# Four engines round the first weight unit, the mixing norm in two token parts, and token rows that start at 32 bytes

## The reference

```python
def rms_norm(x, g):
    xf = x.astype(jnp.float32)
    y = xf * lax.rsqrt(jnp.mean(xf * xf, axis=-1, keepdims=True) + EPS)
    return (y * g.astype(jnp.float32)).astype(x.dtype)

h = jnp.concatenate([meta, x], axis=1)
xn = rms_norm(h, norm_gains[layer, 0])
proj = xn @ w_in[layer]
...
mixed = (jax.nn.sigmoid(g_a) * y_a + jax.nn.sigmoid(g_b) * y_b) @ w_out[layer]
h = h + rms_norm(mixed, norm_gains[layer, 1])
xn = rms_norm(h, norm_gains[layer, 2])
u = causal_depthwise_conv(xn @ w_up[layer], conv_w[layer], conv_b[layer])
u_gate, u_val = jnp.split(u, 2, axis=-1)
ffn = (jax.nn.gelu(u_gate, approximate=True) * u_val) @ w_down[layer]
```

## Time and profile before

| | us |
|---|---|
| three runs, median (lowest to highest) | 2176.37 (2175.43 to 2178.03) |
| the profiled execution | 2177.4 |
| its span, first to last instruction | 2175.6 |
| TensorE busy in it | 2143.6 |
| VectorE / ScalarE / GpSimd busy | 994.2 / 756.6 / 1010.3 |
| TensorE's share of the chain that ended last | 82% |

### The profile page before, as it was taken

The page is one execution under the profiler, slowest core; times in us unless marked ns, Lnnn a source line. Parts: engine busy times, 40 slices in busy tenths (PEclk is TensorE's granted clock), DMA queues, the critical chain, the costliest instruction groups (busy, mean ns, idle before and its releaser), DMA issues.

```text
span 2175.6 us, 31348 instructions
## 1 busy us (share of the span) xinstructions
PE 2143.6 (99%) x12490; PEld 1848.4 (85%) x12490; DVE 994.2 (46%) x1459; ACT 756.6 (35%) x1018; POOL 1010.3 (46%) x825
## 2 busy tenths in 40 slices
PE   8999999999999999999999999999999999999998
PEld 7897999999999887888888788878788888888886
DVE  5144454379888207322200829671876442222027
ACT  4133455243222216322212415551336332222134
POOL 4322223455555547555544545254331555555444
PEclk9999999999999999999999999999999999999999
DMA  4321111212222223322222221114220222222222
GB/s 165 103 69 69 59 44 74 97 59 97 96 92 83 108 95 111 120 96 96 97 97 96 102 101 44 57 60 153 78 78 21 97 97 97 96 96 97 96 101 93
DMA packets 31950, 195.17 MB, mean 90 GB/s; under 512 B 3968, under 2 KB 4480, under 8 KB 10096
## 3 DMA queue, kind: packets, MB, share of 16 engines
q1 hardware_dynamic: 26352, 182.66, 23.4%
q10 hardware_dynamic: 5504, 11.18, 1.6%
HBM read 189.47 MB, written 4.23 MB: 89 GB/s over the span
## 4 chain that ended last, share of the span: by engine, by line
PE 82%; issue 7%; DVE 5%; POOL 4%; ACT 1%; DMA 0%; SPq 0%; DVEq 0%; POOLq 0%; ACTq 0%
PE ps L2377 72%; POOL wlo L709 4%; PE ps L2972 2%; DVE sqa L1527 1%; PE ps L3187 1%; PE ps L3171 1%; PE ps L3054 1%; DVE x2lo L1515 1%; PE ps L3107 1%; PE ps L2656 1%; PE ps L2679 0%; PE ps L3152 0%; PE ps L2715 0%; PE ps L3197 0%; DMA h<-h 0%
## 5 line engine op out<-in xcount | busy, mean ns | idle before, releaser
L709 POOL TENSOR_TENSOR wlo<-raw,whi 128x512 fp32r<-128x512 f32 (+2 forms) x820 | 1009.0, 1263 | 1139.4 <-ACT whi L775 1035.4
L775 ACT CAST whi<-raw 128x2048 fp32r<-128x2048 f32 x162 | 309.6, 1911 | 810.7 <-PE ps L2377 753.3
L2377 PE MATMUL ps<-x2hi,whi 128*128 128x512 f32 x1136 | 448.9, 395 | 1.2 <-DVE x2lo L1515 1.1
L2377 PE MATMUL ps<-x2hi,wlo 128*128 128x512 f32 x1136 | 442.6, 390 | 0.0
L2377 PE MATMUL ps<-x2lo,whi 128*128 128x512 f32 x1136 | 442.4, 389 | 0.0
L2377 PE MATMUL ps<-xhi,whi 128*128 128x256 f32 (+2 forms) x1336 | 271.5, 285 | 12.2 <-DVE xlo L1581 9.3
L2377 PE MATMUL ps<-xlo,whi 128*128 128x256 f32 (+2 forms) x1336 | 270.0, 284 | 0.0
L2377 PE MATMUL ps<-xhi,wlo 128*128 128x256 f32 (+2 forms) x1336 | 269.9, 283 | 0.0
L2377 PEld LDWEIGHTS ps<-x2hi,whi 128*128 128x128 f32 x1136 | 213.4, 188 | 49.6 <-issue 4.8
L2377 PEld LDWEIGHTS ps<-x2lo,whi 128*128 128x128 f32 x1136 | 213.5, 188 | 44.6 <-issue 1.7
L2377 PEld LDWEIGHTS ps<-x2hi,wlo 128*128 128x128 f32 x1136 | 213.3, 188 | 44.3
(11 more groups left out here) (472 smaller groups left out, 2759.9 us busy)
## 6 DMA issues: line engine op xcount, KB each, us to landing
raw<-wstream SPq DMA_DIRECT2D x170, 1024.0 KB, 4.8
h<-h SPq DMA_DIRECT2D x4, 528.0 KB, 8.7
ncb<-c_rows ACTq DMA_DIRECT2D x8, 256.0 KB, 3.5
ple_rows<-ple_out ACTq DMA_DIRECT2D x4, 512.0 KB, 4.0
bias<-bias_rows ACTq DMA_DIRECT2D x8, 256.0 KB, 4.6
ple<-ple_rows ACTq DMA_DIRECT2D x4, 512.0 KB, 5.5
out_dram<-outb SPq DMA_DIRECT2D x8, 256.0 KB, 2.9
raw<-wstream ACTq DMA_DIRECT2D x4, 256.0 KB, 7.3
```

The costliest lines, as they stand in the source:

```text
L709: return nc.gpsimd.tensor_tensor(wlo[b][:, cols], raw[b][:, cols], whi[b][:, cols].bitcast(F32), ALU.subtract)
L775: nc.scalar.copy(whi[b][:], raw[b][:]).then_inc(sig("hi_done"), 1)
L2377: ins = mm(dst, w[slot][:, cols], xx(tok), start=first and p_ == 0, stop=last and p_ == 2, skip_group_check=True)
```

## The change

Four things change.

1. The first unit. The gain column of each chunk travels in front of the tokens, in 32 columns (128 bytes, `HG`) ahead of chunk 0, so `h` begins 128 bytes later, as does all that lies behind it. `h` comes in five parts (chunks 0, 1, 2, 3-4, 5-7), the first weight unit in three, and the constants move from ScalarE's queue to the end of SyncE's. ScalarE loads its function table before its first wait and then does only the first quarter of `whi` and all eight `xhi`; GpSimd copies the other three quarters of `whi`; VectorE does the unit's `wlo`. TensorE runs ten products of a zeroed tile with itself, an eleventh, and then alternates: the high product of chunk k, then the two others of chunk k-1. The second unit is copied and split in quarters.
2. The mixing norm. The five column sums lie in two banks, for blocks 0-1 and 2-4; mean, power and spreading are done for each part by itself. ScalarE copies the root once, whole. TensorE gets ten filler products (`keep_busy`, 512 columns each, into a free bank) between its waits.
3. `fhi`/`flo` start at column 8 (32 bytes in), and `yhi`/`ylo` are the same rows.
4. With that, `first_high` of the second unit is done before the second half of the first.

```diff
@@
-X_FROM = 12
-Y_FROM = 30
+X_FROM = 8
+HG = 32
@@
-        h = at("h", [P, KC, T1])
+        hg = at("hg", [P, HG + KC * T1])
+        h = hg[:, HG:].rearrange("p (k t) -> p k t", t=T1)
+        x_loads = [(0, 1), (1, 2), (2, 3), (3, 5), (5, KC)]
@@
-        yhi, ylo = (rows[:, :, Y_FROM:Y_FROM + TN] for rows in x_rows)
+        yhi, ylo = fhi, flo
@@ SyncE
-            sp.dma_start(cv[:], cvec).then_inc(sig("gains_in"), 16)
-            for q in range(4):
-                sp.dma_start(h[:, 2 * q:2 * q + 2, :], h0[:, 2 * q:2 * q + 2, :]).then_inc(sig(f"h_in{q}"), 16)
+            for n, (a, z) in enumerate(x_loads):
+                cols = slice(HG + a * T1 if a else 0, HG + z * T1)
+                sp.dma_start(hg[:, cols], h0[:, cols]).then_inc(sig("part_in3" if n == 4 else f"h_in{n}"), 16)
             sp.dma_start(raw[1][:], wstream[1]).then_inc(sig("raw_ready1"), 16)
+            sp.dma_start(fw0[:], fw).then_inc(sig("consts_in"), 16)
...
@@ GpSimd
+            for q in range(1, 4):
+                cols = slice(q * BANK, (q + 1) * BANK)
+                if q < 3:
+                    pool.wait_ge(sig(f"part_in{q}"), 16)
+                pool.wait_ge(sig("hi_first"), q)
+                nc.gpsimd.tensor_copy(whi[0][:, cols], raw[0][:, cols]).then_inc(sig("hi_first" if q < 3 else "hi_done"), 1)
+            pool.wait_ge(sig("lo_done"), 1)
...
                     if u == U_UP + 1:
-                        pool.wait_ge(sig("norm_mean"), 1)
-                        nc.gpsimd.tensor_tensor(mix_root, mix_mean, half_col.to_broadcast([P, 5]), ALU.pow).then_inc(sig("norm_root"), 1)
+                        for part, (a, z) in enumerate(MIX_PARTS):
+                            pool.wait_ge(sig("norm_mean"), part + 1)
+                            nc.gpsimd.tensor_tensor(mix_root[:, a:z], mix_mean[:, a:z],
+                                                    half_col.to_broadcast([P, z - a]), ALU.pow
+                                                    ).then_inc(sig("norm_root"), 1)
@@ ScalarE
+            nc.scalar.preload_act_table_set("natural_log_exp_and_others")
+            act.wait_ge(sig("part_in0"), 16)
+            nc.scalar.copy(whi[0][:, 0:BANK], raw[0][:, 0:BANK]).then_inc(sig("hi_first"), 1)
+            for n, (a, z) in enumerate(x_loads):
+                act.wait_ge(sig("part_in3" if n == 4 else f"h_in{n}"), 16)
+                for k in range(a, z):
+                    nc.scalar.activation(xhi[:, k, :], h[:, k, :], ACT.Copy, scale=hg[:, k:k + 1]
+                                         ).then_inc(sig("xhi_ready"), 1)
@@ VectorE
             for k in range(KC):
+                if k % 2 == 0:
+                    q, cols = k // 2, slice(k * HALF, k * HALF + BANK)
+                    dve.wait_ge(sig("hi_first" if q < 3 else "hi_done"), q + 1 if q < 3 else 1)
+                    vec.tensor_tensor(wlo[0][:, cols], raw[0][:, cols], whi[0][:, cols].bitcast(F32), ALU.subtract
+                                      ).then_inc(sig("lo_first" if q < 3 else "lo_done"), 1)
                 dve.wait_ge(sig("xhi_ready"), k + 1)
@@ TensorE
+            pe.wait_ge(sig("cols_ready"), 1)
+            idle_turns(10)
+            pe.wait_ge(sig("hi_first"), 1)
+            idle_turns(1)
+            for k in range(KC + 1):
+                if k < KC:
...
+                    pe.wait_ge(sig("xhi_ready"), k + 1)
+                    for c in range(2):
+                        high_tile(k, c)
+                if k >= 1:
...
+                    pe.wait_ge(sig("x_ready"), k)
+                    for c in range(2):
+                        ins = low_tile(k - 1, c)
...
+            for part in range(2):
+                part_sums(sq_sum1, part, True)
+            pe.wait_ge(sig("hi_done"), U_UP + 1)
+            keep_busy(2, 2)
+            pe.wait_ge(sig("sq_done"), 2 * KC)
+            part_sums(sq[1], 0, False).then_inc(sig("norm_half"), 1)
+            part_sums(sq[1], 1, False).then_inc(sig("total_done"), 1)
+            keep_busy(4, 2)
```

More of the change, by code:

```diff
@@ L259, in build @@
         madds = masks_r[:, P:2 * P]
+        idle = at("idle", [P, HALF], offset=arena)
         ntri_r = at("ntri_r", [P, P], F32R, offset=temp + 14720)
@@ L868, in _ @@
+            act.wait_ge(sig("gains_in"), 16)
             nc.scalar.copy(fwh[:], fw0[:, 0:KC * 8]).then_inc(sig("fw_hi"), 1)
@@ L2463, in v_tail, with idle_turns, high_tile, low_tile @@
                 return ins
+            def idle_turns(n):
+                for _ in range(n):
+                    mm(bank(7)[:, 0:HALF], idle[:, 0:P], idle[:], start=True, stop=True)
+            def high_tile(k, c):
+                for dst, tok in wide_places(STAGE1[c]):
+                    ins = mm(dst, whi[0][:, (2 * k + c) * P:(2 * k + c + 1) * P], xhi[:, k, tok], start=k == 0,
+                             stop=False, skip_group_check=True)
+                return ins
+            def low_tile(k, c):
+                cols = slice((2 * k + c) * P, (2 * k + c + 1) * P)
+                for w, xx, last in ((whi, xlo, False), (wlo, xhi, k == KC - 1)):
+                    for dst, tok in wide_places(STAGE1[c]):
+                        ins = mm(dst, w[0][:, cols], xx[:, k, tok], start=False, stop=last, skip_group_check=True)
+                return ins
@@ L2747, in _ @@
             pe.wait_ge(sig("sq_added"), adds_before(2))
-            for src, first in ((sq_sum1, True), (sq[1], False)):
-                if not first:
-                    pe.wait_ge(sig("sq_done"), 2 * KC)
-                for j, t in enumerate(MIX_BLOCKS):
-                    ins = mm(mix_sums[:, j:j + 1], src[:, t:t + P], one_col, start=first and j == 0,
-                             stop=not first and j == 4, skip_group_check=True)
-            ins.then_inc(sig("total_done"), 1)
-            norms[0] += 1
@@ new lines, in part_sums @@
+            def part_sums(src, part, first):
+                a, z = MIX_PARTS[part]
+                for j in range(a, z):
+                    ins = mm(mix_sums[part][:, j - a:j - a + 1], src[:, MIX_BLOCKS[j]:MIX_BLOCKS[j] + P], one_col,
+                             start=first and j == a, stop=not first and j == z - 1, skip_group_check=True)
+                return ins
+            for part in range(2):
+                part_sums(sq_sum1, part, True)
+            pe.wait_ge(sig("hi_done"), U_UP + 1)
@@ new lines, in _ @@
+            keep_busy(2, 2)
[3 more added lines that the diff above has]
+            keep_busy(4, 2)
+            norms[0] += 1
+            pe.wait_ge(sig("mix_ready"), 4)
+            for part, (first, last) in enumerate(MIX_PARTS):
+                pe.wait_ge(sig("norm_root"), part + 1)
+                for j in range(first, last):
+                    n = P if j < 4 else TN - 4 * P
+                    ins = mm(mix_scale[:, j * P:j * P + n], mix_root[:, j:j + 1].to_broadcast([P, P]), ident[:, P - n:],
+                             start=True, stop=True, skip_group_check=True)
+                ins.then_inc(sig("log_done" if part else "norm_half"), 1)
+                keep_busy(2, 2)
```

131 lines of the change are left out of this document (61 added, 70 removed).

## The result

The change made the kernel slower: 2210.19 us (median of 4 runs, 2208.46 to 2211.14) against 2176.22 us (4 runs, 2175.43 to 2178.03), a ratio of 1.0154 with an interval of 1.0143 to 1.0166. I had forecast 2170.8 us. The profiled execution took 2210.66 us, its span is 33.3 us longer than that of before.

What follows compares the result with a forecast made beforehand. TensorE was taken as the bound, busy 2143.6 of 2175.6 us. Gains of 3.1 (first unit), 0.65 (mixing norm), 0.9 (projection) and 1.0 (FFN), together 5.65 us, gave 2170.8 us; range for 8 in 10: 2166.5 to 2176.5.

Steps and rivals of the forecast that it cites:

- the sentence on the other weight tiles: Some 2,000 tiles streaming 512 columns, rows starting on a multiple of 128 bytes before and after, keep their pace: no change.
- the sum: Gains of 3.1 + 0.65 + 0.9 + 1.0 = 5.65 us, giving a median of 2170.8 us.
- Rival B: The whole row address counts; the 128-byte shift puts the FFN at a slow place: 2177.7 or 2181 us; chance 0.15.
- Its own sign: In the FFN, a tile time of 0.725 us or more would decide for the slow-address rival.
- Part 1: First unit: zero products and earlier supply start real products at 8.3 us; gain 3.1 us, bounds 0.8 to 3.9.
- Part 2: Mixing norm: two-part root and filler products let dense FFN work begin earlier; gain 0.65 us.
- my bound of 0.5: Mixing norm: a loss of 0.5 us if the second part delays the root's copy more than fillers win back.
- Part 3: Token rows starting at 32 bytes: gain 0.9 us in the output projection and 1.0 us in the FFN.
- D: The address of the rows does nothing and the differing paces are chance: 2172.6 us; chance 0.08.
- A: 32 bytes is the fast place, all FFN tiles at 0.700: 2167.8 us, or 2167 with the projection; chance 0.2.
- C: First unit: zero products don't raise the clock, or supply comes later than thought: 2173.1 to 2175 us; chance 0.12.

Runs made afterwards that it cites:

- the second experiment: Kernel before with 128 unused bytes ahead of the weight buffers, so weights and rows both lie 128 bytes later: 2177.1 us, ratio 1.0003.

## Why the prediction was wrong, point by point

**The step that failed** is the sentence on the other weight tiles: rows "that start on a multiple of 128 bytes before and after" and so "keep their pace". A multiple of 128 was not enough. The distance from the weights went from 0 to 128, and 5952 products became 5.66 ns slower, 33.7 us where the sum had nothing. Rival B came near the mechanism (it blamed the rows' address, and the second experiment shows the distance), but I priced it on the FFN's tiles alone (5.1 to 8 us), the one place where the rows vary, and not on the products that make most of the kernel. Its own sign, an FFN tile of 0.725, did not come either: it was 0.720. "" showed that place matters; the untouched rows showed one pace at one distance, which says nothing of another. The honest bound for a shift of all rows would have been that spread, 0.700 to 0.740 or 6%, over all products; 2.5% a product of 512 columns and 1.5% of the time came true.

**Part 1** was right: 2.86 us measured for 3.1, real products at 8.25 for 8.3, unit 0 done at 20.46 for 20.0, and the end set by VectorE's adds (19.09 to 26.7, said: 19.1 to 26.5). Not seen was that with that cover gone the products of zeros are worth nothing.

**Part 2** was right in size (0.7 for 0.65) where the clock stays up. In the profiled execution of the change it lost 0.4: the loss lies within my bound of 0.5, but I had laid that to the copy of the root, and it was the fillers ahead of the spreading, at half clock, that did it. GpSimd's power of a part took 0.77 us, between the bounds of 0.6 and 1.17.

**Part 3**, the two priced terms. The projection was to go to 0.713 (0.9 us): it is 0.720 in the change and 0.710 at distance 0. The FFN was to go to 0.710 (1.0 us): it is 0.720 in the change, a loss of 2.0 us, and 0.710 at distance 0, with 0.9 us to gain against the old rows. The value was right, but partly by luck: it was taken from the middle between rows of 0.700 and 0.7145.

**The rivals.** D is refuted. In the formula of the Trainium skill's page "TensorE: Matmul & The Clock Gate", section "Back-to-back issue gap", the gap depends on columns and clock alone; here the same product at the same clock has 226.7 to 233.3 ns, so the measurement decides against it. A is refuted at 32 bytes (0.710 at best); its pace of 0.700 exists throughout the loop at a distance of 176. C is refuted: the clock rose, and the supply came in time.

**The sum.** With the distance restored, the parts give 2.8 + 0.7 + 1.1 + 1.0 = 5.6 us where I had 5.65, the spans show 5.2 and the medians 3.9. In the traces the terms can be followed: 2.8 us ahead at the sum of squares, 3.8 at the end of the projection (442.89 against 446.66), 5.2 at the end. All but the one step held, within some tenths of a microsecond.

## What to carry to other kernels

A buffer that is made longer moves all that lies behind it, and in this kernel the pace of the products depends on how far the streamed rows lie from the weight tile. Where buffers feed TensorE, pad by a multiple of 256 bytes, the step that gave the pace back here, or compare the start-to-start time of an untouched loop afterwards. Read a pace in more than one place of a loop: here it changed at a wait. When a trace shows a dependence one can't explain, price it over all work that the edit moves, not only over the work where it was seen. And before warming an engine's clock, see whether another engine ends later anyway.

## What the runs showed of the hardware

- A product of 512 columns in fp32 pieces takes 226.7 ns at a distance of 0 modulo 256 bytes between streamed and stationary operand, 228.9 at 64, and 232.4 to 233.3 at 32, 128, 192 and 224. At 128 it is shown that the distance counts and not the place of the rows or of the weights; at 64 and 192 the stretch with exchanged roles fits this; at 32 and 224 only the rows were moved.
- Tiles of 256 and 258 columns have their own order in the FFN's loop: 0.710 us at 32, 0.720 at 160, 0.700 at 176. At 48 one execution holds two or three paces out of 0.700, 0.710 and 0.713, and goes from one to the other at a wait; at 224 two stages of one kernel had 0.710 and 0.720.
- Products of zeros bring TensorE to its faster pace like others: with them the first real pairs are 0.245 us apart, without them 0.44. In a stretch with short waits and fillers the granted clock fell to 0.50 in two traced versions and stayed at 1.00 in the others with the same instructions there; ten executions of one version fall in two groups 1.2 us apart.
- A GpSimd copy of 128x512 in the first unit of the change took 0.83 us (1.65 for two in a row; 0.96 for the first), where its subtractions of that size before took 1.26 and 1.50.
